# First block of a two-block network on one core: other orders between its heads' steps, fewer root passes on VectorE, casts at other places, two kinds of small DMA issued by SP

## What is computed

```python
def first_block(x, ...):                   # x: 1 x 256 tokens x 1024
    for l in range(2):
        g = norm_gains[l]
        h = rms_norm(x, g[0])
        if l % 2 == 0:                     # "even": two mixers side by side
            qa, fa, ia, ga, xb, yb = split_cols(h @ even_w_in[e], EVEN_SIZES)
            oa = hgrn2_mix(qa, fa, ia, ga, ...)   # 4 heads, gated linear attention, chunks of 64
            ob = rglru_mix(xb, yb, ...)           # 4 groups of 128 channels, a linear recurrence
            mix = concatenate([oa, ob]) @ even_w_out[e]
        else:                              # "fox": attention with forget gates, 16 heads
            qc, kc, vc, fc = split_cols(h @ odd_w_in[o], ODD_SIZES)
            mix = fox_attention(qc, kc, vc, fc + fox_f_bias[o]) @ odd_w_out[o]
        x = x + rms_norm(mix, g[1])
        h = rms_norm(x, g[2])
        x = x + rms_norm(conv_ffn(h, ...), g[3])   # "ffn0", "ffn1"
```

## Time and profile before

| | |
|---|---|
| median of three runs | 1667.36 us |
| profiled execution: time / span | 1674.56 / 1672.6 us |
| TensorE (matmul) busy | 1597.8 us, 96% |
| VectorE / ScalarE busy | 1072.5 us (64%) / 831.1 us (50%) |
| granted TensorE clock, mean | 0.987 |
| even mixer with its seam in, ffn0, fox, ffn1 | 0 to 130, 130 to 337, 337 to 480, 480 to 713 us |

### The profile page before, as it was taken

One profiled execution on the slowest core, in us unless ns is written; L12 is line 12 of the kernel. 1 busy time (PEld: TensorE's weight loads), 2 busy tenths in 40 slices (PEclk: granted clock), 3 DMA queues, 4 the chain that ended last, 5 costly groups with the idle time before them and its releaser, 6 DMA issues.

```text
span 1672.6 us, 23419 instructions
## 1 busy us (share of the span) xinstructions
PE 1597.8 (96%) x9108; PEld 1341.7 (80%) x9108; DVE 1072.5 (64%) x1990; ACT 831.1 (50%) x1517; POOL 154.9 (9%) x148
## 2 busy tenths in 40 slices
PE   7988999989989999989999999999999999999998
PEld 7977999878778888867768877787788878787877
DVE  6687777785768778764573656515547855455665
ACT  5855555555656555532303455633336364545564
POOL 0110111210000304100000010100003000000000
PEclk9999999999999999989999999999999999999999
DMA  7536655553355544434401111124522314233333
GB/s 253 175 106 220 218 189 182 183 190 114 115 177 184 181 141 152 163 103 162 164 1 63 51 51 39 57 83 153 178 98 101 114 63 139 81 121 101 101 113 126
DMA packets 61886, 217.70 MB, mean 130 GB/s; under 512 B 7888, under 2 KB 8144, under 8 KB 61648
## 3 DMA queue, kind: packets, MB, share of 16 engines
q1 hardware_dynamic: 58608, 212.40, 37.5%
q10 hardware_dynamic: 3168, 3.80, 0.7%
HBM read 215.09 MB, written 1.05 MB: 129 GB/s over the span
## 4 chain that ended last, share of the span: by engine, by line
PE 66%; DVE 13%; ACT 10%; issue 8%; POOL 2%; ACTq 1%; DMA 0%; DVEq 0%; POOLq 0%
PE PS L344 18%; PE PS L346 17%; PE PS L345 17%; DVE WL L311 3%; ACT WH L294 3%; PE PS L2768 2%; PE PS L2074 2%; PE PS L2083 2%; POOL AR L1590 2%; PE PS L502 1%; PE PS L2148 1%; PE PS L821 1%; PE PS L2125 1%; DVE X L475 1%; PE PS L1927 1%
## 5 line engine op out<-in xcount | busy, mean ns | idle before, releaser
L311 DVE TENSOR_TENSOR WL<-RAWB,WH 128x1024 fp32r<-128x1024 f32 x345 | 425.5, 1238 | 230.8 <-ACT WH L294 225.2
L344 PE MATMUL PS<-RH,WH 128*128 128x256 f32 (+1 forms) x1560 | 505.3, 324 | 15.7 <-DVE WL L311 4.2
L345 PE MATMUL PS<-RH,WH 128*128 128x256 f32 (+1 forms) x1560 | 493.4, 316 | 0.0
L346 PE MATMUL PS<-RH,WL 128*128 128x256 f32 (+1 forms) x1560 | 493.0, 316 | 0.0
L294 ACT CAST WH<-RAWB 128x1024 fp32r<-128x1024 f32 x346 | 358.4, 1041 | 227.1 <-PE PS L346 173.0
L344 PEld LDWEIGHTS PS<-RH,WH 128*128 128x128 f32 x1560 | 300.9, 193 | 50.7 <-issue 13.4
L344 PE MATMUL PS<-WH,RH 128*128 128x512 f32 (+1 forms) x768 | 305.1, 397 | 11.6 <-DVE WL L311 6.7
L346 PEld LDWEIGHTS PS<-RH,WL 128*128 128x128 f32 x1560 | 300.8, 193 | 18.6
L345 PEld LDWEIGHTS PS<-RH,WH 128*128 128x128 f32 x1560 | 301.2, 193 | 18.0 <-issue 0.2
L345 PE MATMUL PS<-WL,RH 128*128 128x512 f32 (+1 forms) x768 | 296.6, 386 | 0.0
L346 PE MATMUL PS<-WH,RH 128*128 128x512 f32 (+1 forms) x768 | 296.4, 386 | 0.0
(11 more groups left out here) (358 smaller groups left out, 1645.9 us busy)
## 6 DMA issues: line engine op xcount, KB each, us to landing
RAWB<-ws SPq DMA_DIRECT2D x394, 512.0 KB, 3.5
TMP<-gains ACTq DMA_DIRECT2D x8, 256.0 KB, 3.1
CS<-cs SPq DMA_DIRECT2D x1, 1472.0 KB, 8.8
X<-x SPq DMA_DIRECT2D x2, 512.0 KB, 3.9
X<-ctx SPq DMA_DIRECT2D x2, 512.0 KB, 8.3
AR<-dec ACTq DMA_DIRECT2D x2, 512.0 KB, 7.1
out<-X SPq DMA_DIRECT2D x4, 256.0 KB, 2.0
AR<-rgw SPq DMA_DIRECT2D x1, 512.0 KB, 5.0
```

What stands on the lines that cost most here:

```text
L311: eng.e.tensor_tensor(k.WL[:, i % SPL, :], k.RAWB[:, i % RAW, :], k.WH[:, i % SPL, :].bitcast(F32), ALU.subtract).then_inc(*eng.done("wl", i))
L344: pe.e.matmul(o, wh, xh, start=first, stop=False)
L345: pe.e.matmul(o, wh, xl, start=False, stop=False)
L346: return pe.e.matmul(o, wl, xh, start=False, stop=last)
```

## The change

- **Seams.** The high part of the next layer's first chunk is cast before the second half's squares instead of after them; in the four seams of the first block up to ffn1's, both first chunks are cast before the eight high parts, and VectorE makes all eight rests before the second chunk's rest. In the very first seam a third chunk is cast and split before the gates' small constants are made.
- **Even mixer.** ScalarE no longer takes V and the scores behind all four recurrences; recurrences 2 and 3 move to steps `r20` and `r30` between the heads' steps; a table load moves from before V to after the scores; head 0's sum of squares goes ahead of tile 1. The root of a head takes three passes on ScalarE (one more) and two on VectorE (two fewer).
- **ffn0 and ffn1.** The table for gelu is loaded at the start of the layer instead of at the first gelu.
- **Fox.** In each round the scores go before the turn and the output, on all engines.
- **SP.** The norm rows and the fox sums are issued by SP between its weight loads, the sums of pair j after the seventh chunk past pair j-1's keys.

```diff
@@ seam_act
-        cast_to(k, act, m.opens(k))
+            cast_to(k, act, m.opens(k))
+        cast_to(k, act, m.opens(k) + (not m.shift))
@@ seam_dve
-            if n == 3:
+            if n == (3 if m.shift else 7):
                 rest_to(k, dve, m.opens(k) + 1)
@@
-              "h01 h11 t00 h02 h21 h12 h31 t10 h03 h22 h13 h32 t20 h04 h23 h33 h14 t30 h24 t40 h34".split()]
+              "h01 h11 t00 r20 h02 h21 h12 r30 h31 h03 t10 h22 h13 h32 h23 t20 h04 h33 h14 t30 h24 t40 h34".split()]
+def head_root_act(k, act, s):
+    b, act_ = k.ps.of(s, "ss")[:, 0:256], act.e.activation
+    r, q = k.rb.take(act, s, "r")[:, 0:256], k.vv.take(act, s, "v")[:, 0:256]
+    act.wait_ge(*k.PE.at(s, "ss"))
+    act_(r, b, ACT.Ln, bias=k.c_eps, scale=1.0 / 128).then_inc(*act.done())
+    act.wait_ge(*act.last())
+    act_(r, r, ACT.Exp, scale=-0.5).then_inc(*act.done())
+    act.wait_ge(*act.last())
+    act_(q, r, ACT.Square).then_inc(*act.done(s, "r0"))
+def head_root_dve(k, dve, s):
+    r, q, b = k.rb.of(s, "r")[:, 0:256], k.vv.of(s, "v")[:, 0:256], k.ps.of(s, "ss")[:, 0:256]
+    dve.wait_ge(*k.ACT.at(s, "r0"))
+    dve.e.scalar_tensor_tensor(q, b, 128 * EPS, q, ALU.add, ALU.mult).then_inc(*dve.done())
+    k.ps.free(dve, s, "ss")
+    dve.wait_ge(*dve.last())
+    dve.e.scalar_tensor_tensor(r, q, -3.0 * 128, r, ALU.add, ALU.mult).then_inc(*dve.done(s, "r"))
+    k.vv.free(dve, s, "v")
@@ even_act
     seam_act(k, act, seams(k)[s])
+    cast_to(k, act, k.ws.opens(s, "f", 0) + 2)
@@
-    act.e.preload_act_table_set(LNEXP)
     cast_to(k, act, v0 + 5)
+    def high(j):
+        act.wait_ge(*k.DVE.at(s, "rgout", j))
+        act_(L.Y[0][:, 4 + j, :], L.I[:, j, :], ACT.Copy).then_inc(*act.done(s, "yh", 4 + j))
+    high(0)
     for n in range(2):
         act.wait_ge(*k.PE.at(s, "v", n))
...
-    for j in range(4):
-        act.wait_ge(*k.DVE.at(s, "rgout", j))
-        act_(L.Y[0][:, 4 + j, :], L.I[:, j, :], ACT.Copy).then_inc(*act.done(s, "yh", 4 + j))
-        scores(j)
-    cast_to(k, act, k.ws.chunk(s, "v", 0) + 2)
+    scores(0)
+    scores(1)
+    high(1)
+    scores(2)
+    scores(3)
+    act.e.preload_act_table_set(LNEXP)
@@ even_dve
-    rest_to(k, dve, v0 + 4)
-    recurrence(2)
     rest_to(k, dve, v0 + 5)
     turned_keys(0)
     turned_keys(1)
-    recurrence(3)
+    low(0)
     turned_keys(2)
     turned_keys(3)
-    for j in range(4):
-        low(j)
-    rest_to(k, dve, k.ws.chunk(s, "v", 0) + 2)
+    low(1)
@@ ffn_act
+    act.e.preload_act_table_set(GELU)
@@
-FOX_STEPS = [(r - d, p) for r in range(20) for d, p in ((0, 0), (0, 4), (3, 2), (4, 3), (2, 1))
+FOX_STEPS = [(r - d, p) for r in range(20) for d, p in ((0, 0), (0, 4), (2, 1), (3, 2), (4, 3))
@@ sp_program
+    gains = {k.ws.chunk("even", "out") + 3: 0}
+    for n, first in enumerate((("ffn0", "up", 0), ("fox", "fc"), ("ffn1", "up", 0))):
+        gains[k.ws.opens(*first) + 6] = n + 1
+    sums = {k.ws.chunk("fox", "v", 1, 0) + 5: (0, 1)}
+    for j in range(2, 8):
+        sums[k.ws.chunk("fox", "kp", j - 1) + 7] = (j,)
```

More of the change, by code:

```diff
@@ L21 @@
 LNEXP = "natural_log_exp_and_others"
+GELU = "gelu_apprx_tanh_and_others"
 def param_layout():
@@ L929, in seams, with gains_sp @@
             "end": Seam("odd2", None, None)}
-def gains_act(k, act, n):
+def gains_sp(k, sp, n):
+    if n:
+        sp.wait_ge(*k.DVE.at(("even", "ffn0", "fox")[n - 1], "x", 1, 1))
+    else:
+        sp.wait_ge(*k.DVE.at("even", "gated", 3))
     for h in range(2):
-        act.e.dma_start(k.T[4 + h][:, :], k.gains[n, :, half(h)]).then_inc(k.s_gain, 16)
+        sp.e.dma_start(k.T[4 + h][:, :], k.gains[n, :, half(h)]).then_inc(k.s_gain, 16)
 EVEN_STEPS = [(u[0], int(u[1]), int(u[2])) for u in
-              "h01 h11 t00 h02 h21 h12 h31 t10 h03 h22 h13 h32 t20 h04 h23 h33 h14 t30 h24 t40 h34".split()]
+              "h01 h11 t00 r20 h02 h21 h12 r30 h31 h03 t10 h22 h13 h32 h23 t20 h04 h33 h14 t30 h24 t40 h34".split()]
 def even_tile(i):
     return (i + 4) % 8
+def head_root_act(k, act, s):
[15 more added lines that the diff above has]
+    k.vv.free(dve, s, "v")
 class Even:
@@ L1048, in even_pe @@
             back(n)
-        elif p < 4:
+        elif kind == "h" and p < 4:
             head(n, p)
@@ L1138, in even_act @@
             out_ahead(k, act, s, [h], cast_to)
+        elif kind == "r":
+            high(h)
         elif p == 2:
@@ L1146, in even_act @@
         elif p == 3:
-            rstd_act(k, act, (s, h), 256, 128, True)
+            head_root_act(k, act, (s, h))
         elif p == 4:
@@ L1185, in even_dve @@
     seam_dve(k, dve, seams(k)[s])
+    rest_to(k, dve, k.ws.opens(s, "f", 0) + 2)
     dve.wait_ge(k.s_pr, 16)
@@ L1314, in even_dve @@
             out_ahead(k, dve, s, [h], rest_to)
+        elif kind == "r":
+            recurrence(h)
+            low(h)
         elif p == 1:
@@ L1329, in even_dve @@
         elif p == 3:
-            rstd_dve(k, dve, (s, h), 256, 128)
+            head_root_dve(k, dve, (s, h))
             dve.wait_ge(*dve.last())
@@ L1452, in ffn_act @@
     s = L.s
+    act.e.preload_act_table_set(GELU)
     if l == 1:
         filter_loads_act(k, act, 0)
-    act.wait_ge(*k.DVE.at(("even", "fox")[l], "x", 1, 1))
-    gains_act(k, act, 2 * l + 1)
     for j, p in FFN_STEPS:
@@ L1626, in stats, with sums_sp @@
     return (k.SM[:, 64 + 4 * i + n:64 + 4 * i + n + 1] for n in range(3))
+def sums_sp(k, sp, j):
+    L, s = Fox(k), "fox"
+    sp.wait_ge(*k.DVE.at(s, "sums"))
+    sp.wait_ge(*k.POOL.at(s, "ones"))
+    sp.wait_ge(*k.PE.at(s, "S", 2 * j - 3, 1))
+    for n, (r, rk, rq) in enumerate(HEAD_ROWS):
+        Q, K = L.QK[j % 2][n]
+        g = 2 * j + n
+        sp.e.dma_start(K[rk:rk + 1, :], L.Lb[g:g + 1, :]).then_inc(k.s_sums[j % 2], 16)
+        sp.e.dma_start(Q[rq:rq + 1, :], L.Lb[g:g + 1, :]).then_inc(k.s_sums[j % 2], 16)
 def fox_pe(k, pe):
@@ L1702, in fox_act @@
             k.ps.free(act, s, "v", c, n)
[L1704 to L1716, removed]
     for h, p in FOX_STEPS:
@@ L1737, in fox_act @@
                     *act.done(s, "exp", h, qb))
-            if par and j < 6:
-                sums(j + 2)
         elif p == 2:
@@ L3214, in sp_program @@
                 e.dma_start(k.X[:, 2 + i, :], k.ctx[i]).then_inc(k.s_x[2 + i], 16)
+        if c in gains:
+            gains_sp(k, sp, gains[c])
+        for j in sums.get(c, ()):
+            sums_sp(k, sp, j)
         if c == 6:
```

6 lines of the change are left out of this document (2 added, 4 removed).

## The result

The kernel after takes 1649.34 us (median of four runs, 1647.92 to 1654.54), the one before 1667.86 us beside it: a ratio of 0.9896 with an interval of 0.9874 to 0.9917, 18.5 us less. The forecast was 1648.4. Its total was right, but partly by luck: two terms came out 3.4 us short and one 2.3 us over, and one that was met (the first part of the mixer's tail) was met with 1.5 us of clock that its own steps don't hold. One profiled execution further down, the first of e10, ran with a mean granted clock of 0.654 for 2247.79 us and is read no further.

A forecast was written before the change was run, and what follows sets the result against it. TensorE's own work plus its waits bound the kernel; 1.8 + 4.0 + 2.4 + 1.1 + 3.6 + 6.1 = 19.0 us off the 1667.4 median gives 1648.4 us; range 1645 to 1652, with rivals 1643 to 1657.

The forecast's parts named there:

- First seam: Start of the kernel: unbroken input rests start the second projection at 17.4 us, the third at 20.3; gain 1.8 us.
- Even mixer's tail: V projection to output: earlier scores bring tile 1 2.0 us sooner, shorter roots help up to tile 5; gain 4.0 us.
- rival 4: More than counted: the clock also stays up in the even mixer's tile 0, worth 1.6 us; 1646.5 us, chance 0.06.
- Norm rows: Even mixer's tail: rows behind a chunk in SP's queue may land just when the seam wants them; 0.1 us off.
- rival 3: SP becomes the bound: each fox pair's chunk comes late behind the scores' wait; 1692 us, chance 0.04.
- Seams: Into ffn0, fox and ffn1: unbroken input rests start the second projection 0.8 us sooner in each; gain 2.4 us.
- Table load in ffn0: Gelu's table loaded at the layer's start, where ScalarE has free time, removes a TensorE wait; gain 1.1 us.
- Fox start: Without eight small DMAs on ScalarE the cast comes 4 us sooner, the wait goes, clock recovers; gain 3.6 us.
- Fox rounds: Without DMAs and with scores first, both waits at the turn go, pairs fall from 10.16 to 9.15 us; gain 6.1.
- Rival 2: Fox rounds keep their period: turn's copies behind ScalarE's exponentials hold the pair's output; gain 0 to 2 us, chance 0.12.
- SP: Issues the fox sums at 2.4 us a pair plus waiting, hidden by later casts; uncovered they would cost 19 us.
- The Trainium skill's drain: Even mixer's tail: 1.38 us of drain behind a table load would make the gain 2.6 us instead of 4.0.

The follow-up runs named there:

- e10: Kernel after, but in odd heads' fox rounds ScalarE makes the next chunk's cast before the high part of the pair's output: ratio 0.9861.
- e6: Kernel after with the casts and rests of all seams where they were before: 1658.76 us, ratio 0.9935.
- e4: Kernel after with the even mixer's order from before (recurrences, scores, table load), new roots kept: 1656.98 us, ratio 0.9921.
- e3: Kernel after with the first norm rows asked for one chunk sooner in SP's order: 1649.92 us, ratio 0.9883.
- e5: Kernel after with the heads' old roots (two passes on ScalarE, four on VectorE), new order kept: ratio 0.9916.
- e0: The kernel before, profiled once more with no edit: ratio 0.9998, ten executions from 1666.46 to 1676.82 us.
- e7: Kernel after without the table load at the start of ffn0 and ffn1, so it comes at the first gelu: ratio 0.9904.
- e1: Kernel after with the fox sums issued by ScalarE again, scores still first: 1661.16 us, ratio 0.9950.
- e2: Kernel after with the old order in the fox rounds (turn and output ahead of the scores), sums still by SP: 1646.67 us, ratio 0.9852.
- e11: The same kernel as e10, run and profiled once more: 1648.82 us, ratio 0.9863.

## Why the prediction was right, and where it was not

- **First seam**: 1.8, as forecast (e6 loses 1.7), but by two sizes that cancel: the third projection came at 20.74 us and not at 20.3, and the fourth one's wait, taken at 0.4, did not come.
- **Even mixer's tail**: 4.0 forecast, 3.1 measured. Beyond the first seam, after gains 2.2 us up to tile 1 (2.0 said) and 2.2 from tile 1 to tile 5 (2.1 said), and loses 1.3 from there to the first diagonal (0.1 said).
  - *Up to tile 1* the number was met by luck. The forecast's own steps, scores 1.8 sooner and then 1.3 of waiting for head 3's states, make 0.5 and not 2.0. Measured are 1.9 and 0.97. The rest is mostly the clock, which stayed up in tile 0: 21 matmuls in 3.40 us against 14 in before, which is worth about 1.5 us. That is rival 4, at 0.06, and it goes with the wait that the new order removed (e4).
  - *Norm rows*: "may land just when the seam wants them", taken at 0.1, cost 1.5 in this trace (e3) and 0.2 to 1.3 in the others. The forecast named their place behind a chunk, and in rival 3 the ring order, but did not work out when they land. With the rows on time (e3) the tail gains 4.65 us, 1.5 of it clock.
  - Order and roots were both needed (e4 loses 2.7 us, up to 1.5 of it clock, and e5 1.3).
- **Seams**: 2.4 forecast. At equal clock they are worth about 1.0, 0.4 and 1.1 us (e0, e3, e6), 2.5 in all; the 4.7 measured hold 2.2 us of clock. In the seam into ffn0 the clock went against after: it ran 6.8 us at 0.50 from 129.10 us, where before fell for 3.4 us. That is a fall at a place where the clock had held, which the forecast named as a sign of being wrong; in the other profiles of the new kernels it lasts 3.4 us or (e5) is missing. In fox TensorE gains less: it then waits 0.78 us for a modulation row (L835 at 344.69), a wait that neither before nor e6 has. The long diagonal waits stayed at 3.0 us, as said, but for 2.44 us in the seam into ffn0 of after, at half clock.
- **Table load in ffn0**: right (1.2 us; e7).
- **Fox start**: 3.6 forecast, 3.4 measured, as 2.2 for the wait and 1.2 for the clock (e1).
- **Fox rounds**: the step that failed. "Without the DMAs, and with the scores ahead of the turn, both waits go" is half right. Without the DMAs they go and bring 8.8 us (e2), more than the 6.1 that I called TensorE's idle time and took for the bound. I had set the work of a pair at the 9.15 busy us of the trace, and it is 8.7. With the scores ahead they come back in part and cost 5.2 us. Rival 2 named the right engine, ScalarE and its strict order, but neither what is held nor what holds it: not the output behind the turn's copies, but the next cast behind the output's high part (e11). With 3.6 us the rounds lie nearer its 0 to 2 than my 6.1.
- **SP**: hidden, as said; 0.6 us for each issue, and no landing of `RAWB` among TensorE's waits in fox.
- **The Trainium skill's drain** of 1.38 us behind a table load ("ScalarE: Activation LUTs", What ACT_TABLE_LOAD costs) was a rival price for the tail. The trace speaks against it here: the tail's own load starts at 92.21 us and the next cast at 93.51, and in ffn0 the cast starts 1.29 us after the load at 138.39, with nothing between.
- **The sum** was taken off the median and not off the profiled execution, and that was needed: e0 gives the same waits and a span 7.2 us shorter. Off 1674.56 it would have been 1655.6.
- **The range**: the terms' lower bounds, with 1.1 and 6.1 for the two that have none, add up to 13.5 us, which is 1653.9 and not 1652; and the rounds, the term that missed most, had no bound in it.

Together: the forecast left out 1.4 us of loss by the rows, put the rounds 2.5 us too high and the way to tile 1 by about 1.3; against that stand 1.5 + 2.2 + 1.2 = 4.9 us of clock where 1.6 were counted. The total was right because these nearly cancel. Of the clock part the 1.5 us in tile 0 came back with the wait in e4; the other 3.4 us rest on falls that differ between executions of one kernel.

## What to carry to other kernels

When work leaves an in-order engine, read what now stands between it and the late engine's next instruction: here a cast moved ahead of one copy won 3.9 us, where the whole DMA move was worth 8.8. Don't change the order in the same step as the engine, unless each is timed alone. And a DMA moved into a queue of large loads has to be asked for by its landing time, not by its issue.

## What the runs showed that was not expected

- The idle time in front of a waiting matmul understates the wait: two waits of 1.01 us together cost 1.45 us a pair, because the matmuls' overlap is lost too. A pair that keeps TensorE fed shows 8.71 busy us, the same work with waits 9.15.
- Executions of one kernel lay up to 10 us apart, with the granted clock (1666.46 at 0.994, 1676.82 at 0.986). Some falls came back at the same places, others did not: the wait of 2.2 us before tile 0 was followed by one in three profiles of three, the wait of 1.97 us at the start of fox in both profiles of before, and not in e1.
- Two norm rows of 256 KB took 3.8 us from the first issue to the last landing in ScalarE's own queue (before, 119.68 to 123.47), and between the weights in SP's queue 6.1 us in after (114.97 to 121.05), 5.0 and 4.7 with the same place in e2 and e11, and 4.5 when they were asked for one chunk sooner (e3, 112.57 to 117.11).
